# Position bias rows written to DRAM during the recurrence, in two halves

## The reference, cut to what matters

```python
BAND, CHUNK, MAX_REL = 576, 64, 256          # LEFT_CHUNKS = 8
def chunk_band_attend(q, k, v, rel_table):   # rel_table: 8 heads x 513
    rel = (jnp.arange(CHUNK)[:, None] + LEFT_CHUNKS * CHUNK) - jnp.arange(BAND)[None, :]
    idx = jnp.clip(rel, -MAX_REL, MAX_REL) + MAX_REL
    bias = rel_table.astype(jnp.float32)[:, idx]
    ...
        sc = jnp.einsum('bqhd,bkhd->bhqk', qc, kb) * scale + bias[None]
```

## Time and profile before

| | us |
|---|---|
| median of three runs | 2397.83 (2397.09 to 2399.01) |
| the profiled execution | 2400.04 |
| its span, first to last instruction | 2398.2 |

### The profile page before, as it was taken

One profiled execution on the slowest core, in us unless ns is written; L12 is line 12 of the kernel. 1 busy time (PEld: TensorE's weight loads), 2 busy tenths in 40 slices (PEclk: granted clock), 3 DMA queues, 4 the chain that ended last, 5 costly groups with the idle time before them and its releaser, 6 DMA issues.

```text
span 2398.2 us, 41197 instructions
## 1 busy us (share of the span) xinstructions
PE 2210.3 (92%) x17720; PEld 1572.6 (66%) x17720; DVE 1142.6 (48%) x2011; ACT 710.7 (30%) x1086; POOL 217.9 (9%) x97
## 2 busy tenths in 40 slices
PE   7989898989989999988989999989899999799994
PEld 5485858585436889665668888857655677456563
DVE  4545454553756555245567773252355643511113
ACT  2323222321221222344353332242134532322221
POOL 0020202020000000000124344410000000000001
PEclk9999999999989999999999999989999999899997
DMA  8201010102547556101323332345120133579994
GB/s 256 83 9 37 20 37 20 36 21 83 158 153 231 178 182 200 38 1 48 111 82 94 87 104 80 97 80 145 31 79 19 45 110 96 206 288 397 398 412 171
DMA packets 216314, 295.26 MB, mean 123 GB/s; under 512 B 7640, under 2 KB 191872, under 8 KB 207968
## 3 DMA queue, kind: packets, MB, share of 16 engines
q1 hardware_dynamic: 210784, 274.85, 33.9%
q0 software_dynamic: 3072, 9.74, 2.0%
q10 hardware_dynamic: 2304, 8.39, 0.9%
HBM read 279.84 MB, written 13.11 MB: 122 GB/s over the span
## 4 chain that ended last, share of the span: by engine, by line
PE 79%; DVE 8%; DMA 6%; ACT 4%; issue 2%; SPq 1%; POOL 0%; POOLq 0%; DVEq 0%; ACTq 0%
PE ps L661 11%; PE ps L1148 10%; PE ps L766 10%; PE ps L989 8%; PE ps L957 6%; PE ps L1179 5%; PE ps L1359 4%; DMA ring<-in_w_up 3%; PE ps L1013 3%; PE ps L1043 2%; PE ps L870 2%; PE ps L1059 2%; PE ps L1332 2%; PE ps L1130 2%; PE ps L1206 2%
## 5 line engine op out<-in xcount | busy, mean ns | idle before, releaser
L766 PE MATMUL ps<-arena 64*64 64x64 f32 x7168 | 227.3, 222 | 15.4 <-POOL arena L1915 8.8
L766 PEld LDWEIGHTS ps<-arena 64*64 64x64 f32 x7168 | 222.3, 138 | 20.0 <-POOL arena L1915 9.6
L661 PE MATMUL ps<-hT,ring 128*128 128x512 f32 (+1 forms) x480 | 213.0, 600 | 3.1 <-ACT hT L1431 2.4
L1921 POOL TENSOR_TENSOR w_low<-ring,w_high 128x2048 fp32r<-128x2048 f32 x22 | 101.8, 4627 | 817.0 <-ACT w_high L1674 817.0
L661 PEld LDWEIGHTS ps<-hT,ring 128*128 128x128 f32 (+1 forms) x480 | 90.0, 189 | 120.4 <-issue 117.7
L1148 PE MATMUL ps<-h_high,w_low 128*128 128x512 f32 x352 | 140.8, 400 | 5.7 <-DVE h_low L2336 5.7
L1148 PE MATMUL ps<-h_high,w_high 128*128 128x512 f32 x352 | 140.8, 400 | 0.0
L1148 PE MATMUL ps<-h_low,w_high 128*128 128x512 f32 x352 | 139.3, 396 | 0.0
L2242 DVE CUSTOM_DVE_ANT_0 arena<-ps,arena 128x256 f32<-128x256 f32 (+3 forms) x160 | 67.0, 468 | 124.5 <-PE ps L1059 124.4
L1457 ACT ACTIVATE arena<-ps 128x512 f32<-128x512 f32 x104 | 62.1, 597 | 209.7 <-PE ps L766 199.4
L2059 DVE TENSOR_TENSOR arena<-ps,arena 128x512 f32<-128x512 f32 x88 | 60.8, 691 | 119.1 <-PE ps L766 119.0
(11 more groups left out here) (408 smaller groups left out, 4362.6 us busy)
## 6 DMA issues: line engine op xcount, KB each, us to landing
ring<-in_w_in SPq DMA_DIRECT2D x54, 1024.0 KB, 5.3
arena<-in_w_ada SPq DMA_DIRECT2D x80, 512.0 KB, 4.2
arena<-in_w_down SPq DMA_DIRECT2D x32, 1024.0 KB, 9.3
ring<-in_w_gate SPq DMA_DIRECT2D x30, 1024.0 KB, 9.8
ring<-in_w_up SPq DMA_DIRECT2D x30, 1024.0 KB, 11.2
ring<-in_w_up SPq DMA_DIRECT2D x44, 512.0 KB, 4.9
ring<-in_w_down SPq DMA_DIRECT2D x8, 1024.0 KB, 5.1
y_scratch<-arena ACTq DMA_DIRECT2D x16, 512.0 KB, 7.4
```

The lines of the kernel that those rows point to most:

```text
L661: mm = pe.matmul(dst, w[:, k, hf * P:hf * P + width], rhs(k), start=(start and k == 0), stop=(stop and k == kts - 1))
L766: mm = pe.matmul(ps[r, bank, cc], l[r, cc], x[r, 0:64] if x is eye64 else x[r, cc], start=(i == 0), stop=(i == len(terms) - 1))
L1921: pool.tensor_tensor(W_LOW[:, slot_, :], ring[:, slot_, :], W_HIGH[:, j % 2, :].bitcast(F32), ALU.subtract).then_inc(w_low, 1)
```

## The change

The rows get eight partitions of 320 words of their own (`BIAS_ROW`), so their use no longer waits for a free stretch of the large arena. The load, the fill and the write move to POOL's program in the recurrence, one part at the start of each round's masks; since the buffer holds only half a row, the row goes out in two writes of 8 x 128 x 320 words. What stays at `in2` is a wait on a semaphore for both writes and the skewed read, now behind the loads of the chunk mask and the positions alone.

```diff
-        BROW = area(33280, 640)
+        BIAS_ROW = sb("bias_row_half", [P, 320])[0:8, :]
@@ gpsimd
+            def bias_part(q):
+                if q == 0:
+                    pool.dma_start(BIAS_ROW[:, 255:320], a["rel_reversed"][:, 0:65]).then_inc(bias_row, 16)
+                if q == 1:
+                    pool.wait_ge(bias_row, 16)
+                    pool.tensor_copy(BIAS_ROW[:, 0:255], BIAS_ROW[:, 255:256].broadcast_to([8, 255])).then_inc(pool_link, 1)
+                    pool.wait_ge(pool_link, 1)
+                    pool.dma_start(a["bias_scratch"][:, :, 0:320], BIAS_ROW.unsqueeze(1).broadcast_to([8, P, 320])).then_inc(bias_out, 16)
+                if q == 2:
+                    pool.wait_ge(bias_out, 16)
+                    pool.dma_start(BIAS_ROW, a["rel_reversed"][:, 65:385]).then_inc(bias_row, 16)
+                if q == 3:
+                    pool.wait_ge(bias_row, 32)
+                    pool.dma_start(a["bias_scratch"][:, :, 320:640], BIAS_ROW.unsqueeze(1).broadcast_to([8, P, 320])).then_inc(bias_out, 16)
             for q in range(4):
+                bias_part(q)
                 for li, b in enumerate(LEVELS):
@@ gpsimd, at the start of in2
             pool.wait_ge(half_done, 2 * FIRST["in2"])
             pool.wait_ge(freed["D"], BEFORE["in2"]["D"])
-            pool.dma_start(BROW[0:8, 255:640], a["rel_reversed"][:, 0:385]).then_inc(bias_row, 16)
             pool.dma_start(CH, ...).then_inc(got_pos, 16)
             pool.dma_start(ANG[:, 3, :].bitcast(I32), ...).then_inc(got_pos, 16)
-            pool.wait_ge(bias_row, 16)
-            pool.tensor_copy(BROW[0:8, 0:255], BROW[0:8, 255:256].broadcast_to([8, 255])).then_inc(pool_link, 1)
-            pool.wait_ge(pool_link, 1)
-            pool.dma_start(a["bias_scratch"], BROW[0:8, :].unsqueeze(1).broadcast_to([8, P, 640])).then_inc(bias_out, 16)
-            pool.wait_ge(bias_out, 16)
+            pool.wait_ge(bias_out, 32)
             pool.dma_start(BT, bass.AP(a["bias_scratch"].tensor, 127, [[639, P], [P * 640, 8], [1, T]])).then_inc(got_bias, 16)
```

## The result

| | before | after |
|---|---|---|
| median, us | 2398.42 (2397.09 to 2400.28, 4 runs) | 2430.28 (2423.51 to 2434.88, 4 runs) |
| the profiled execution, us | 2400.04 | 2423.51 |
| its span, us | 2398.2 | 2421.6 |

What follows compares the result with a forecast made beforehand. The prediction took PE's wait at `in2` for a weight load stretched by POOL's bias write as the bound; -8.7 + 0 + 0 + 0 = -8.7 us gave 2391.3 us profiled, 2389.1 us median, range 2386.5 to 2394.

Steps and rivals of the forecast that it cites:

- What bounds the kernel: At the start of `in2`, PE waits for tile 4's weight load, stretched from 5.3 to 29.4 us by POOL's bias write.
- the 8.7 us of `in2`: Gain at `in2` once the write leaves: 5.76 us of PE standing still plus 2.98 us of slow clock, forecast as -8.7 us.
- The skewed read 60 us earlier: At `in2`, the read moves from 1642.91 to about 1583.6; 0 to 1 us on the norm, taken as 0.
- POOL's instructions, and its waits: In the recurrence, POOL's load, copy and issues, 2 us in a gap of 102, cost nothing.
- The length of the writes: Two writes in the recurrence: 27.8 us each if packets cost by bytes, 55.6 if by piece; 28 taken, cost 0 us.
- the arithmetic of the stretched load: Tile 4's load at `in2`: 64 packets per engine, each taking turns with a write packet, 64 x (0.40 + 0.05) = 29 us.
- what remains beside the writes: PE's instruction fetches in the recurrence, one per 3.75 us, 1.2 us each, taken as undisturbed by the writes: 0 us.
- 0.07: Chance given to a slower kernel through PE's instruction stream or something like it, about 2414 us.
- The sign that I had named: The forecast is wrong if PE's recurrence rounds grow beyond 120 us.
- The writes starve PE of instructions: Rival in the recurrence: fetches take 6.6 us instead of 1.2, PE loses 25 us, total about 2414 us; chance 0.07.
- +16 forecast: Net change if instruction fetches in the recurrence are stretched: -8.7 + 25 = +16 us, giving 2414 us.
- The deciding point: In the recurrence, PE loses time from the point where an instruction fetch takes more than 3.75 us.

Runs made afterwards that it cites:

- kernel without writes: Changed kernel with both bias writes and their waits taken out, the skewed read taking its 2 MB from `w_down`: 2393.41 us, 0.9971 of the kernel before.
- wide write at `in2`: Kernel before, its one 640-word write kept at `in2` but from 128 partitions, behind the chunk-mask and positions loads: 2393.41 us (0.9967), again 2393.54 us (0.9957).

## Why the prediction was wrong, point by point

**What bounds the kernel, and the 8.7 us of `in2`.** Right. The load of tile 4 was held back by the write on half of the engines, the split did become the next to be late, 6 us before it was needed, evictions follow each other by 11.2 us, and 8.71 us came back. The kernel without writes and the wide write at `in2` show the gain as a whole: 8.7 us lie inside the interval of each.

**The skewed read 60 us earlier.** Right: it is issued at 1615.71, and the stretch from DVE's last residual to PE's first full-speed tile is 29.26 us (1613.22 to 1642.48), before 29.05 (1580.21 to 1609.26).

**POOL's instructions, and its waits.** Right: hidden, as the kernel without writes shows.

**The length of the writes.** 28 us taken, 29.7 and 30.8 measured. It goes by bytes. One figure on the way was wrong, and with it the arithmetic of the stretched load: I divided the queue's time by 1040 packets, but about half of these are under 512 bytes. The data packets of the old write are of 5 KB and take some 0.8 us, not 0.40. Between 160 and 170 in the changed kernel:

```profile
DMA packets 339, 0.42 MB, mean 42 GB/s; under 512 B 264, under 2 KB 264, under 8 KB 336
q0 software_dynamic: 336, 0.37, 38.6%
q8 instruction: 3, 0.05, 1.9%
```

72 packets above 2 KB with 0.37 MB, 0.386 x 16 x 10 / 72 = 0.86 us each at most, since the 264 small ones have a part of that time. With 0.8 us in place of 0.40 the sum of turns would be 64 x (0.8 + 0.05) = 54 us, not 29. That 64 x 0.45 us met the 29.4 us was luck. The load was held until the write was over: from its issue at 1616.55 to 1642 there was time for some 31 turns of 0.8 us, and what was left went through behind the write, 423 packets of weights from 1642 to 1643.5, with the landing at 1645.93. So the write did stretch the load, but by what remained of it and not by 64 turns.

**The step that failed: "what remains beside the writes".** I read from the earlier trace rows that a fetch beside the old write took 0.96 us, no longer than alone, and costed the fetches at nothing. The share of a queue is the time that its packets took once they were being served. It holds no waiting. The changed kernel shows the same figure while PE was starving:

```profile
q0 software_dynamic: 94, 0.48, 48.5%
q8 instruction: 1, 0.02, 0.6%
```

This is from 425 to 435, one fetch of 0.006 x 16 x 10 = 0.96 us, and PE stood through all of it. The warning was in my own text: the held weight load's packets had a short time of their own, 0.054 us, and the load still took 29.4 us instead of 5.3. The second half of the error is that the old write's neighbour was a stretch of 128x512 multiplications, which needed one fetch between 1620 and 1630, where the recurrence needs one per 3.75 us; PE would not have shown a fetch that was 13 us late. The moved write ran beside a consumer that the trace of before never had beside it, and 0.07 was too little for that. The sign that I had named came: the masks of rounds 2 and 3 stand 144.6 us apart (396.93 to 541.57), where a round of the kernel before took 121.

**The rival that came true.** "The writes starve PE of instructions" named mechanism and place. Its price was 25 us for the stops, and 28.3 came, but the nearness is luck: it was built from 8.5 fetches of 6.6 us that cost 2.9 us each, and what came were three fetches that cost 6.4 to 13.1 us each, with the others undisturbed. What it left out is the clock, 8.4 us in the profiled execution: +16 forecast, +23.5 measured there. Over four runs the median is 7 us above the profiled one, with a spread of 11 us, where before's is 3. That the number of fetches caught changes from run to run would explain it; only one execution was profiled, so this is not shown. The deciding point "a fetch takes more than 3.75 us" was right as a condition for long, but the number to compare is the transfer's length with the 7 us until PE stands.

**How a fetch gets its turn.** The Trainium skill ("DMA: Bandwidth & Descriptors", "Issuing engines are not separate DMA queues") says that all queues share the 16 engines; the runs agree, since writes on either queue held up fetches. It also says that an engine takes turns by packet ("Queues, rings and completion order"). I had taken that for one packet of the profile, here 0.8 us. The runs speak against that reading for a fetch: the stops of full writes are 6.4 to 13.8 us, and they are hardly shorter with packets of a quarter of the size. But the same section puts typically 9 to 17 descriptors into a packet. If a "packet" of the profile is one such descriptor, which no run here shows, an estimate from that figure and 0.8 us is a turn of 7 to 14 us, near the stops. On SyncE's queue, with some 0.2 us for each row, it would need more of them. So the rule isn't refuted, only my use of it. Why one fetch waits for so long no run here settles; the profile shows when a fetch was served, but neither on which engine nor when it was asked for.

## What to carry to other kernels

Before a long transfer is moved to a stretch where the DMA queues are idle, look at what else lives on the DMA engines there: PE's instruction stream is the one thing that no load list shows, and the stretch of 64x64 multiplications here had only 5 to 7 us of it ahead. The share of a queue in the trace is service, not waiting, so a short packet time beside a long transfer is no proof that nobody waits; ask whether the neighbour would have shown it. And before moving a slow transfer, make it fast: spread over 16 engines and 128 source partitions instead of 8 and 8, the write went from 55.6 to 9.8 us, and there was no need to move it.

## What the runs showed of the hardware

- A write to DRAM of 1280 KB took 30.2 us from 8 partitions, 15.5 us from 16 and 6.5 us from 128: the first step is the number of engines, the second the number of partitions that each engine reads from (the write's queue took 47% of the time of 16 engines, then 91% and 97% in the middle of the write). The Trainium skill ("DMA: Bandwidth & Descriptors", "Rules for kernel authors") says that an outermost dimension of c below 16 confines a transfer to at most c engines; the 46% in the earlier trace rows and the halving agree. That 16 engines with a partition each are 2.4 times slower than with eight each is not in that rule.
- PE's instructions come in fetches of 16 KB (one serves about 250 instructions, 125 multiplications of 64x64 with their weight loads). With all engines held it stood still 6.3 to 7.2 us after the issue of the transfer, six times out of six, and in the changed kernel it went on 1.4 to 1.6 us after a fetch had landed. The Trainium skill ("Runtime: NRT & Kernel Launch", "Instruction fetch mechanics") has the blocks of 16 KiB and a buffer of 2048 instructions for PE, eight blocks; at 3.75 us each that would be a reserve of 30 us, by an estimate from its figure, and the runs show none beyond 5 to 7 us. The same section says that the next page is fetched while the current one is executed, and with that the runs agree.
- The stops come whether the hardware queue or POOL's software queue carries the transfer (7.7 and 13.8 us against 8.8 and 19.5).
